# First gate and up tiles accumulated in eighths as pairs of modulation columns arrive

## What is computed

```python
mod = (jax.nn.silu(c) @ w_ada[l] + b_ada[l]).reshape(B, N_MOD, D)   # N_MOD 9, D 1024
m = [mod[:, j] for j in range(N_MOD)]
h = modulate(rmsnorm(x, ffn1_pre_g[l]), m[0], m[1])   # h * (1 + scale) + shift
y = swiglu(h, ffn1_w_gate[l], ffn1_w_up[l], ffn1_w_down[l])
x = x + 0.5 * m[2][:, None, :] * rmsnorm(y, ffn1_post_g[l])
```

## Time and profile before

| | us |
|---|---|
| median of 3 runs | 2249.75 (2248.67 to 2251.26) |
| the profiled execution, its own time | 2255.79 |
| its span | 2254.1 |
| TensorE busy | 1995.6 (89%) |
| VectorE busy | 1292.9 (57%) |
| ScalarE busy | 633.4 (28%) |
| GpSimd busy | 616.5 (27%) |
| first matmul of `gate_up(0)` | 42.00 |
| last matmul of `gate_up(0)` ends | 196.05 |

### The profile page before, as it was taken

How to read it: one execution, slowest core, us unless ns; L and a number is a source line. 1 busy time by engine, 2 the same in 40 slices (tenths; PEclk the granted TensorE clock), 3 DMA queues, 4 the chain that set the end, 5 groups by cost and what they waited for, 6 DMA issues and landing times.

```text
span 2254.1 us, 20010 instructions
## 1 busy us (share of the span) xinstructions
PE 1995.6 (89%) x6128; PEld 1074.0 (48%) x6128; DVE 1292.9 (57%) x3368; ACT 633.4 (28%) x1519; POOL 616.5 (27%) x554
## 2 busy tenths in 40 slices
PE   3999999899998889899879998888999899777876
PEld 2886477488644344344434443343444444332332
DVE  5550145200024467876576887657687757777764
ACT  2000125300024232453233254313235422222221
POOL 1100000000000133343334343344333334444442
PEclk8999999899999999999989999999999999899999
DMA  9987844444685799999999999999999999999997
GB/s 386 392 345 263 315 170 150 149 153 157 212 280 183 296 420 421 409 413 412 421 402 410 421 421 421 395 418 403 420 421 408 411 421 388 390 421 422 416 416 323
DMA packets 113380, 794.41 MB, mean 352 GB/s; under 512 B 12377, under 2 KB 15961, under 8 KB 18440
## 3 DMA queue, kind: packets, MB, share of 16 engines
q0 software_dynamic: 78912, 574.65, 62.1%
q1 hardware_dynamic: 28944, 207.73, 24.5%
q10 hardware_dynamic: 5432, 10.93, 1.4%
HBM read 792.19 MB, written 4.75 MB: 354 GB/s over the span
## 4 chain that ended last, share of the span: by engine, by line
PE 56%; DMA 22%; DVE 10%; ACT 6%; issue 4%; POOL 1%; POOLq 0%; DVEq 0%; ACTq 0%
DMA wide<-experts_in,pick_idx 20%; PE PS L970 18%; PE PS L1380 17%; PE PS L468 10%; PE PS L1430 6%; DVE wide L1037 3%; PE PS L1625 1%; ACT diag L956 1%; POOL wide L1088 1%; DMA ring<-wts_in 1%; ACT L951 1%; DMA early<-ada_in 1%; PE PS L462 1%; DVE topi L985 1%; DVE topi L988 1%
## 5 line engine op out<-in xcount | busy, mean ns | idle before, releaser
L970 PE MATMUL PS<-wide,diag 128*128 128x512 f32 x2048 | 999.5, 628 | 193.8 <-ACT diag L956 188.3
L1088 POOL DMA_INDIRECT wide<-experts_in,pick_idx x512 | 589.1, 1151 | 1287.9 <-PE PS L970 785.3
L1037 DVE CUSTOM_DVE_ANT_0 wide<-wide,htok 128x1024 f32<-128x1024 f32 x512 | 619.2, 1224 | 245.2 <-DMA wide<-experts_in,pick_idx 238.7
L970 PEld LDWEIGHTS PS<-wide,diag 128*128 128x128 f32 x2048 | 391.1, 198 | 716.1 <-issue 430.0
L1380 PE MATMUL PS<-hT,ring 128*128 128x256 f32 x1744 | 382.7, 382 | 15.1 <-DMA ring<-wts_in 11.4
L1380 PEld LDWEIGHTS PS<-hT,ring 128*128 128x128 f32 x1744 | 333.6, 192 | 64.3 <-issue 16.6
L468 PE MATMUL PS<-ring,hTm 128*128 128x512 f32 (+1 forms) x704 | 326.8, 593 | 1.1 <-ACT hTm L318 0.8
L956 ACT ACTIVATE diag<-cst,coef 128x128 f32<-128x128 f32 x512 | 177.6, 394 | 274.2 <-DVE coef L1048 273.7
L951 ACT ACTIVATE coef<-dots 128x2 f32<-128x2 f32 x256 | 52.2, 204 | 586.3 <-DVE dots L1037 585.6
L468 PEld LDWEIGHTS PS<-ring,hTm 128*128 128x128 f32 x704 | 135.3, 194 | 163.3 <-issue 155.7
L1691 DVE TENSOR_TENSOR actT<-silu,PS 128x256 f32<-128x256 f32 (+1 forms) x44 | 18.5, 421 | 231.7 <-ACT silu L1220 231.7
(11 more groups left out here) (326 smaller groups left out, 1302.0 us busy)
## 6 DMA issues: line engine op xcount, KB each, us to landing
ring<-wts_in SPq DMA_DIRECT2D x191, 1024.0 KB, 5.8
early<-ada_in POOLq DMA_DIRECT2D x36, 1024.0 KB, 8.3
wide<-experts_in,pick_idx POOLq DMA_INDIRECT x512, 12.0
ring<-wts_in SPq DMA_DIRECT2D x8, 780.0 KB, 8.7
strip_t<-strips_one ACTq DMA_DIRECT2D x1, 2048.0 KB, 11.6
strip_dil<-strips_one ACTq DMA_DIRECT2D x1, 1536.0 KB, 19.7
x<-x_in ACTq DMA_DIRECT2D x1, 1024.0 KB, 9.2
bias_t<-strip_t ACTq DMA_DIRECT2D x1, 1024.0 KB, 13.4
```

The lines of the kernel that those rows point to most:

```text
L970: last = pe.matmul(PS[:, ACC + half, :], diag[:, n % RING, :], ups[:, n % RING, half * BANK:(half + 1) * BANK], start=k == 0, stop=k == PI ...
L1037: v.tensor_tensor_reduce(out=downs[:, n % RING, :], in0=downs[:, n % RING, :], in1=htok[:, tb, :], scale=1.0, scalar=0.0, op0=ALU.mult, op ...
L1088: pool.indirect_dma_start(pairs_of_rows[:, k % RING, :, :].rearrange("p c n -> p (c n)"), None, experts.rearrange("l e d -> (l e) d"), bas ...
```

## The change

The two shares of the modulation that the first FFN needs are stored as pairs: `ada` tile c now holds chunk c of the shift and chunk c of the scale, so that after tile c one eighth of `hT` can be made. Five things follow in the code.

1. **VectorE.** `pair_sums(c)` sums the two chunks of pair c, `pair_columns(c)` adds their bias and makes one column of `prea` (`first_cols`). The order is pair sums 0 and 1, normalize, columns 0 and 1, then for c of 2 to 7 sums and columns. Its share of `evacuate(0)` is gone.
2. **ScalarE.** `first_hT(c)` makes each eighth of `hT` for all 256 tokens in one instruction, in the order of the pairs; the strip copies stand between them.
3. **TensorE.** `first_turn` transposes x by eighths into banks 4 to 7. `wave(j, c0, c1)` adds eighths c0 to c1-1 of weight tile j (j of 0 to 2) into bank j. The rest of `gate_up(0)` begins at tile 3. The strips use bank 3 one after the other.
4. **SP.** The wait for 14 chunks is gone; weight tile 0, 1, 2, 3 is issued after 1, 5, 9, 14 chunks.
5. **Constants.** `CONST` is reordered and split: 145 columns (identity, eps, iota) are loaded ahead of `small1`, the other 1280 columns after chunk 16; three late users wait for `consts_loaded` 32.

```diff
-CONST = [("ident", P), ("ones", P), ("tri", P), ("trineg", P), ("hmask", 7 * P), ("iota", K16), ("eps", 1)]
+CONST = [("ident", P), ("eps", 1), ("iota", K16), ("ones", P), ("tri", P), ("trineg", P), ("hmask", 7 * P)]
+EARLY = P + 1 + K16
+WAVE = 3
...
-            sp.wait_ge(m["mod_added"], 2 * ADA_TILES + 6)
             for n in range(TILES):
+                if n <= WAVE:
+                    sp.wait_ge(m["mod_added"], (1, 5, 9, 14)[n])
...
+            act.dma_start(cst[:, 0:EARLY], consts[:, 0:EARLY]).then_inc(m["consts_loaded"], 16)
             act.dma_start(s1[:, :], small1).then_inc(m["smalls_loaded"], 16)
-            act.dma_start(cst[:, :], consts).then_inc(m["consts_loaded"], 16)
...
+            def first_hT(c):
+                act.wait_ge(m["first_cols"], c + 1)
+                act.wait_ge(m["first_turned"], c + 2 - c % 2)
+                act.activation(hT[:, c, :], PS[:, 4 + c // 2, c % 2 * S:(c % 2 + 1) * S], ACT.Identity,
+                               bias=modc[:, c:c + 1], scale=prea[:, c:c + 1]).then_inc(m["first_hT"], 1)
...
+            for c in range(3):
+                first_hT(c)
+            strip(0, HEADS)
+            first_hT(3)
+            first_hT(4)
+            strip(1, A2)
+            for c in range(5, KC):
+                first_hT(c)
             act.wait_ge(m["mod_added"], 16)
+            act.dma_start(cst[:, EARLY:], consts[:, EARLY:]).then_inc(m["consts_loaded"], 16)
...
-            for tb in range(TB):
-                evacuate(0, tb)
...
+            def wave(j, c0, c1):
+                w = tile(FIRST["gu1"] + j)
+                for c in range(c0, c1):
+                    pe.wait_ge(m["first_hT"], c + 1)
+                    for g in range(2):
+                        last = pe.matmul(PS[:, j, g * S:(g + 1) * S], w[:, c * 256 + g * P:c * 256 + (g + 1) * P], hT[:, c, :],
+                                         start=c == g == 0, stop=c == KC - 1, skip_group_check=True)
+                if c1 == KC:
+                    last.then_inc(m["tiles_used"], 1)
...
-                for j in range(4):
+                for j in range(0 if f else WAVE, 4):
                     step(j, 0, True)
...
-            for tb in range(TB):
-                turn(0, tb)
+            first_turn()
+            wave(0, 0, 3)
             pe.wait_ge(m["smalls_loaded"], 16)
             pe.wait_ge(m["strip_loaded"], 16)
...
+            strip(0, "rel", HEADS, 32, "t5")
+            wave(1, 0, 3)
+            for c in (3, 4):
+                wave(0, c, c + 1)
+                wave(1, c, c + 1)
+            strip(1, "rel2", A2, 33, "dil")
+            wave(2, 0, 5)
+            for c in range(5, KC):
+                for j in range(WAVE):
+                    wave(j, c, c + 1)
+            pe.wait_ge(m["strips_copied"], 2)
             gate_up(0)
...
+            def pair_columns(c):
+                v.wait_ge(m["mod_added"], 2 * c + 2)
+                two_ = lambda t: t.rearrange("p (e n) -> p e n", e=2)[:, :, c:c + 1]
+                V(v.tensor_tensor(two_(modc[:, 0:16]), two_(modr[:, 0:16]), two_(o1("b_ada", 0, 16)), ALU.add))
+                v.scalar_tensor_tensor(prea[:, c:c + 1], modc[:, 8 + c:9 + c], 1.0, o1("pre_g", c), ALU.add, ALU.mult)\
+                    .then_inc(m["first_cols"], 1)
...
-            for n in range(8):
-                chunk_of(0, n)
+            pair_sums(0)
+            pair_sums(1)
             v.wait_ge(m["x_loaded"], 16)
             for tb in range(TB):
                 normalize(0, tb)
-            for n in range(8):
-                chunk_of(1, n)
             v.wait_ge(m["smalls_loaded"], 16)
-            columns(0, 2)
-            pre_columns(0)
-            v.sem_inc(m["post_cols"], 1)
-            for tb in range(TB):
-                evacuate(0, tb)
+            pair_columns(0)
+            pair_columns(1)
+            for c in range(2, KC):
+                pair_sums(c)
+                pair_columns(c)
...
+    mods[0:2] = [np.stack([w.reshape(KC, P, D) for w in mods[0:2]], 1).reshape(2 * D, D)]
```

More of the change, by code:

```diff
@@ L144, in program @@
         flat = lambda a: a.rearrange("p a n -> p (a n)")
-        names = """tiles_used x_loaded smalls_loaded consts_loaded strip_loaded x_ready sq_done x_root y_root_fb normed fb_T hT_by_vector
+        names = """first_turned first_cols first_hT tiles_used x_loaded smalls_loaded consts_loaded strip_loaded x_ready sq_done x_root y_root_fb normed fb_T hT_by_vector
             hT_by_scalar c_loaded chunk_loaded c_act mod_added post_cols rows_summed rows_ready strips_summed strips_copied
@@ L732, in mixer_vector @@
                 V(v.tensor_copy(id16, ident))
+                v.wait_ge(m["consts_loaded"], 32)
                 V(v.tensor_copy(neg16, C("trineg")))
@@ L1172, in evacuate @@
             def evacuate(k, tb):
-                act.wait_ge(m["post_cols"], (1, 3, 4)[k])
-                act.wait_ge(m["fb_T"], 4 * k + 2 * tb + 2)
+                act.wait_ge(m["post_cols"], k + 1)
+                act.wait_ge(m["fb_T"], 4 * (k - 1) + 2 * tb + 2)
                 for c in range(4, KC):
@@ L1191, in _, with strip @@
             act.activation(cact[:, :], cact[:, :], ACT.Silu).then_inc(m["c_act"], 1)
+            act.wait_ge(m["x_loaded"], 16)
             act.wait_ge(m["consts_loaded"], 16)
-            act.wait_ge(m["x_loaded"], 16)
             for tb in range(TB):
                 pre(0, tb)
-            act.wait_ge(m["smalls_loaded"], 16)
+            def first_hT(c):
[3 more added lines that the diff above has]
+                               bias=modc[:, c:c + 1], scale=prea[:, c:c + 1]).then_inc(m["first_hT"], 1)
+            def strip(part, rows_):
+                act.wait_ge(m["strips_summed"], part + 1)
+                act.copy(scr1[0:rows_, part * BANK:(part + 1) * BANK], PS[0:rows_, 3, :]).then_inc(m["strips_copied"], 1)
+            for c in range(3):
[6 more added lines that the diff above has]
+                first_hT(c)
             act.wait_ge(m["mod_added"], 16)
+            act.dma_start(cst[:, EARLY:], consts[:, EARLY:]).then_inc(m["consts_loaded"], 16)
             act.dma_start(cst1[:, 2 * BANK:], consts1[:, 2 * BANK:]).then_inc(m["chunk_loaded"], 16)
@@ L1396, in turn, with first_turn, strip @@
                     last.then_inc(m["fb_T"], 1)
+            def first_turn():
+                pe.wait_ge(m["normed"], TB)
+                for c in range(KC):
+                    for tb in range(TB):
+                        a = c % 2 * S + tb * P
+                        last = pe.transpose(PS[:, 4 + c // 2, a:a + P], xn[:, tb, c * P:(c + 1) * P], ident)
+                    last.then_inc(m["first_turned"], 1)
+            def wave(j, c0, c1):
[7 more added lines that the diff above has]
+                    last.then_inc(m["tiles_used"], 1)
+            def strip(part, name, heads, rows_, hot):
+                if part:
+                    pe.wait_ge(m["strips_copied"], part)
+                pe.matmul(PS[0:heads, 3, :], o1(name, 0, heads, rows_), cst1[0:rows_, CC1[hot]:CC1[hot] + BANK],
+                          start=True, stop=True).then_inc(m["strips_summed"], 1)
             def hT_ready(k, tb):
-                pe.wait_ge(m["hT_by_vector"], 2 * k + tb + 1)
-                pe.wait_ge(m["hT_by_scalar"], 2 * k + tb + 1)
+                pe.wait_ge(m["hT_by_vector"], 2 * (k - 1) + tb + 1)
+                pe.wait_ge(m["hT_by_scalar"], 2 * (k - 1) + tb + 1)
             def gain_row(i, bank):
@@ L1442, in _ @@
             pe.wait_ge(m["consts_loaded"], 16)
-            for tb in range(TB):
-                turn(0, tb)
+            first_turn()
+            wave(0, 0, 3)
             pe.wait_ge(m["smalls_loaded"], 16)
             pe.wait_ge(m["strip_loaded"], 16)
-            for bank, name, heads, rows_, hot in ((6, "rel", HEADS, 32, "t5"), (7, "rel2", A2, 33, "dil")):
-                pe.matmul(PS[0:heads, bank, :], o1(name, 0, heads, rows_), cst1[0:rows_, CC1[hot]:CC1[hot] + BANK],
-                          start=True, stop=True).then_inc(m["strips_summed"], 1)
-            for tb in range(TB):
-                hT_ready(0, tb)
+            strip(0, "rel", HEADS, 32, "t5")
[9 more added lines that the diff above has]
+            pe.wait_ge(m["strips_copied"], 2)
             gate_up(0)
             down(0, 0, 0, 10)
-            pe.wait_ge(m["post_cols"], 2)
+            pe.wait_ge(m["post_cols"], 1)
             pe.wait_ge(m["act_ready"], FT)
@@ L1457, in _ @@
             down(0, 0, 10, 11)
-            pe.wait_ge(m["strips_copied"], 2)
             down(0, 1, 0, 8)
@@ L1461, in _ @@
             down(0, 1, 8, 11)
-            pe.wait_ge(m["post_cols"], 3)
+            pe.wait_ge(m["post_cols"], 2)
             pe.wait_ge(m["rows_ready"], 1)
@@ L1601, in _ @@
             pe.wait_ge(m["lru_sq"], 1)
+            pe.wait_ge(m["consts_loaded"], 32)
             chain(PS[:, 6, 0:S], [(C("ones"), scr1[:, 2048 + c * S:2048 + (c + 1) * S]) for c in range(4)])\
@@ L1609, in _ @@
             out_proj(1, 1)
```

(30 more changed lines are left out.)

3 lines of the change are left out of this document (removed).

## The result

The changed kernel takes 2239.95 us in the median of six runs (2234.56 to 2244.68), the kernel before, beside it, 2250.51 us (2247.86 to 2254.46). The ratio is 0.9944, with a 95% interval of 0.9931 to 0.9958: 12.6 us less, 9.5 to 15.5. The prediction was 13.4 us less, 2236.3 us, within 2231 to 2242. The profiled execution has a span of 2232.9 us; it is the fastest of the six, 2234.56 us.

What follows compares the result with a forecast made beforehand. Incoming data was taken to bound the kernel until 42 us, then TensorE. Waves ending at 50.7 us put tile 4 at 58.4 against 71.8 us, 13.4 us earlier: 2249.75 - 13.4 = 2236.3 us median, range 2231 to 2242.

Steps and rivals of the forecast that it cites:

- What bounds the kernel: Until 42 us incoming data sets the time, then TensorE alone through gate and up; the later 14.60 us weight wait moves along.
- Rival (d): Behind the stage, in `down` or the gathers, the gain is given back; 0 to 8 us would remain; chance 0.05.
- Pairs: Modulation loads: fourth pair there at 22 us, pair 7 at 37 us, bounds 32.4 and 39.5 us.
- Normalization: VectorE, before the eighths: 1.8 us of work, at 17 to 20 us, with ScalarE's roots ending near 15.5 us.
- Waves: TensorE's work by eighths on the first three weight tiles: from 29.5 us to 50.7 us, bounds 47 and 56 us.
- from there on TensorE never runs out of work: In the waves from 29.5 us: 21 eighths of 0.864 us and a 1.0 us strip, 19.1 us without gaps.
- The 2.1 us for the clock: At TensorE's start in the waves: the low 1.2 GHz clock costs 2.1 us again.
- rival (a): Lucky arrivals: weight tile 1 at 28 us, no clock loss, tile 4 at 54 us; 18 us gained, 2232; chance 0.11.
- Tiles 3 and 4: Behind the waves: tile 3 without wait to 57.6 us; tile 4's weights at 58.5 us, start 58.4 against 71.8, 13.4 us earlier.
- Debt: Gate and up stage: at 58 us three products and nine chunks outstanding; worked off with 7 us in hand.
- rival (e): Gate and up stage: DMA below both streams' need, tiles above 6.91 us; slower, 2259 us at 0.32 MB/us; chance 0.04.
- The rule on the clock: In the waves: by it the first would cost twice, unnoticed, and a wait inside later ones would lead to 56 us.

Runs made afterwards that it cites:

- waves without early weights: The changed kernel with the four first weight tiles waiting for 14 chunks again; ratio to the kernel before 0.9997 (0.9984 to 1.0011).
- whole constants: The changed kernel with the constants loaded in one piece at the start, behind the small inputs; ratio to the kernel before 0.9950 (0.9930 to 0.9970).
- both edits: The changed kernel with weight tiles after 1, 3, 5, 9 chunks and ScalarE's late loads after the twentieth gate tile; 2236.97 us, ratio to the kernel before 0.9927.
- early weights alone: The kernel before with weight tiles issued after 1, 5, 9, 14 chunks and nothing else; ratio to it 1.0024 (1.0011 to 1.0036), 5.4 us slower.
- the second execution: The changed kernel profiled once more, unedited; span 2241.2 us, 8.3 us more than in its first profiled execution.

## Why the prediction was right

**What bounds the kernel.** Right: `down` moved by 12.2 us, its weight load of 14.6 us with it (14.83), and the matmuls behind the 1.5 us wait, at 392.15 us before, by 11.9. Rival (d) shows at none of these marks; in the whole time the interval of 9.5 to 15.5 us can't exclude a few us of it.

**Pairs.** Pair 7 was put at 37 us with the last column at 40.0; measured 37.3 and 40.07. The run of waves without early weights shows the term behind it, 5.5 us paid by the pairs.

**Normalization.** Put at 17 to 20 us, done from 15.9 to 17.9; the constants were there at 12.8 us. What this is worth the prediction left open. The run with whole constants says 2.55 us at the end of the waves, and 0.9 us on balance behind tile 4.

**Waves.** Put at 50.7 us from 29.5, measured 50.83 from 28.59. The step "from there on TensorE never runs out of work" held in the first execution. In the second it ran out for 1.2 us and arrived at the same time, since it had to wait for weight tile 2 until 37.1 us (put at 36), just where the full clock would have paid. The 2.1 us for the clock were 2.9 in the first execution. The two small misses, start 0.9 us early and clock 0.8 us dearer, cancel, so a miss of only 0.1 us is in part luck: with the same code up to 40 us the waves ended between 50.1 and 51.0 us. What the prediction did not see is that weight tile 2 sets a second bound. It landed at 36.7 us in the first execution and 37.1 in the second, and its stretch of 14 eighths takes 12.1 us at full clock. With this order of issues the waves so can't end before 48.8 us, and the lower bound of 47 us, with rival (a) at 54 us for tile 4, was out of reach.

**Tiles 3 and 4.** Tile 3 without a wait: right (landed near 46.0). Tile 4 at 58.4: measured 59.29, because the tile took 9.9 us from 49.3, and 9.5 was the value chosen. The cause named, the third queue, is shown by the run with ScalarE's late loads behind the twentieth tile.

**Debt.** It held with more room than feared. Product 0 ended at 50.1 us for a tile that started at 59.3, product 4 at 75.6 for 87.0, product 6 at 90.2 for 100.8, and from product 15, at 142.9 us, VectorE waits for silu again. TensorE waited for no product. The least room is 9 us, where the text had 7. From tile 4 on a tile takes 6.91 us as before, so rival (e) did not come.

**The rule on the clock.** The Trainium skill, "TensorE: Matmul & The Clock Gate", section on HAM oscillation, tells of a kernel whose bursts of matmuls are shorter than its waits for data, and in which each burst starts at the low clock. The waits in the waves, 1.2 to 2.3 us, are shorter than the stretches between them, so this case is milder than the page's. The granted clock was 0.50 between 28 and 34 us in the first execution, and 0.58 between 37 and 40 in the second, with 1.00 between 28 and 34, so the trace agrees in part: once in the waves, not behind each wait. Between these two executions it did not decide, because arrivals of weights filled the same time. In the edited kernels it did, by 0.7 us (late loads) and up to 1.7 us (both edits).

**Size.** 13.4 us were forecast, 12.2 us measured at the first `down` matmul, 12.6 us (9.5 to 15.5) in the ratio. Of the missing 1.2 us, 0.9 are tile 4's. The other 0.3 are a reading: the prediction took 71.8 us, the start of ScalarE's silu for tile 3, as the present start of tile 4. TensorE begins tile 4 at 71.5 us, 18 tiles of 6.91 us before 195.89. The median difference, 10.6 us, is compatible with it: six runs of each kernel spread over 7 to 10 us.

## What to carry to other kernels

Where a stretch is bound by a full DMA and the engine that bounds the next stretch idles in it, cut that engine's first work along the axis on which its input arrives, and bring its weights in early enough; neither alone helps, and early weights alone are a loss, since the stream in front pays for them (4.9 us here). Put loads that nobody needs soon out of the stretch in which the first slots are refilled (1.6 us here). Price such a change at a mark directly behind the stage: here it repeats within 1 us, while whole executions differ by 7 to 10.

## What was not expected of the hardware

**A DMA share of 1.00 did not mean that DMA was full.** Between 70 and 120 us the kernel before shows a share of 1.00 at 389 and 386 GB/s, the changed kernel 1.01 and 1.02 at 419 and 423 GB/s, with the same transfers. By the share alone the debt could not have been worked off. The GB/s of a stretch in which a stream is known to be behind is the better ceiling. For the first 35 us of the kernel before, where the prediction read a full DMA from the share, the 6.5 us by which early weights alone put off the last sum are the better evidence.

**In the same wait the clock falls in most executions and holds in one.** Near 380 to 400 us TensorE has short waits of 1.3 to 1.5 us, in both kernels. TensorE's granted clock (PEclk, the value before the DMA share) of the kernel before, 394 to 400 us, and of the two executions of the changed one at the same work, 382 to 388 us:

```profile
394.00:400.00 6.00, 4.72 (x11) 2.29 (x11) 2.55 (x5) 4.74 (x10) 0.00 (x0) 0.50 0.00 0
```

```profile
382.00:388.00 6.00, 4.72 (x16) 2.36 (x16) 2.68 (x5) 4.90 (x10) 0.00 (x0) 1.00 0.00 0
```

```profile
382.00:388.00 6.00, 4.72 (x12) 2.66 (x12) 1.57 (x4) 4.27 (x9) 0.00 (x0) 0.50 0.00 0
```

All three are busy for the same 4.72 of 6 us, and in the first and third TensorE is at 1.2 GHz, in the second at 2.4 GHz. The 16 matmuls right behind the wait take 7.10 us in the second, and 9.02 to 10.11 us in the other nine profiled executions of this document, so it is the first execution of the changed kernel that is the exception. From the end of the 1.5 us wait, at 392.15, 380.21 and 379.03 us, to the start of `gate_up(1)` it is 48.55, 45.78 and 49.94 us: the clock was worth 2.8 us against the kernel before and 4.2 us against the second execution, which had been 1.2 us ahead. This is why the first execution gained 14.7 us at 426 us and only 12.2 us at 184 us. It is no effect of the change.
